# Squared queries of mixer A: turned by transposes in two parts and added up by VectorE, in place of two-column products

## What is computed

```python
q = px[..., :A_WIDTH].reshape(b, t, A_HEADS, HEAD_DIM)
q = apply_axial_rope(rms_norm(q, q_g), cos, sin)          # x tokens
...
s = jnp.einsum('bqkgd,bskd->bkgqs', qi, k_all).astype(jnp.float32) * ATTN_SCALE
p = jax.nn.softmax(s, axis=-1).astype(v_all.dtype)
o = jnp.einsum('bkgqs,bskd->bqkgd', p, v_all)
...
qc = rms_norm((hc @ w_in[:, :A_WIDTH]).reshape(b, lc, A_HEADS, HEAD_DIM), q_g)   # context tokens
```

## Time and profile before

| | |
|---|---|
| median of 3 runs | 1588.56 us (1588.26 to 1594.45) |
| profiled execution, its own time | 1596.21 us |
| its span in the trace | 1594.5 us |
| TensorE busy | 1527.1 us, 96% of the span |
| VectorE, ScalarE, GpSimd busy | 47%, 40%, 43% |
| mean granted TensorE clock | 0.98 of full speed |

### The profile page before, as it was taken

The page is one execution under the profiler, slowest core; times in us unless marked ns, Lnnn a source line. Parts: engine busy times, 40 slices in busy tenths (PEclk is TensorE's granted clock), DMA queues, the critical chain, the costliest instruction groups (busy, mean ns, idle before and its releaser), DMA issues.

```text
span 1594.5 us, 25191 instructions
## 1 busy us (share of the span) xinstructions
PE 1527.1 (96%) x10002; PEld 1231.2 (77%) x10002; DVE 743.1 (47%) x1639; ACT 636.4 (40%) x1337; POOL 686.2 (43%) x661
## 2 busy tenths in 40 slices
PE   5899999999898999999999899999999999999997
PEld 3777777677687888787877677878787877777887
DVE  4435554445534434434355464733332654455154
ACT  3335444444532533333334453434332344444331
POOL 2534444344432533433334445444353535555462
PEclk8999999999999999999999899999999999999999
DMA  9120111112023222222221222213121221111222
GB/s 396 40 80 31 50 54 54 54 58 76 1 99 114 80 73 87 106 80 80 104 83 54 106 87 80 80 53 106 54 79 54 106 106 44 64 54 54 79 86 74
DMA packets 23140, 128.21 MB, mean 80 GB/s; under 512 B 2416, under 2 KB 4592, under 8 KB 9072
## 3 DMA queue, kind: packets, MB, share of 16 engines
q1 hardware_dynamic: 22880, 126.35, 21.9%
q10 hardware_dynamic: 144, 0.26, 0.1%
HBM read 124.50 MB, written 2.10 MB: 79 GB/s over the span
## 4 chain that ended last, share of the span: by engine, by line
PE 84%; DVE 6%; POOL 3%; ACT 3%; issue 2%; DMA 1%; SPq 0%; POOLq 0%; DVEq 0%; ACTq 0%
PE PS L1525 16%; PE PS L1527 16%; PE PS L1526 15%; PE PS L1615 7%; PE PS L1605 6%; PE PS L1641 6%; PE PS L1518 3%; PE PS L1520 3%; PE PS L1519 3%; PE PS L1695 1%; PE PS L1687 1%; POOL WL L2557 1%; DMA XC<-in_xt 1%; PE PS L1538 1%; DVE AR L2354 1%
## 5 line engine op out<-in xcount | busy, mean ns | idle before, releaser
L2557 POOL TENSOR_TENSOR WL<-W,WH 128x512 fp32r<-128x512 f32 x304 | 402.2, 1337 | 322.9 <-ACT WH L1798 322.7
L1525 PE MATMUL PS<-HX,WH 128*128 128x512 f32 (+1 forms) x1008 | 411.8, 408 | 7.4 <-POOL WL L2557 3.6
L1527 PE MATMUL PS<-HX,WL 128*128 128x512 f32 (+1 forms) x1008 | 391.4, 388 | 0.0
L1526 PE MATMUL PS<-LX,WH 128*128 128x512 f32 (+1 forms) x1008 | 391.3, 388 | 0.0
L1525 PEld LDWEIGHTS PS<-HX,WH 128*128 128x128 f32 x1008 | 192.6, 191 | 54.5 <-issue 13.2
L1527 PEld LDWEIGHTS PS<-HX,WL 128*128 128x128 f32 x1008 | 192.1, 191 | 40.1
L2627 POOL TENSOR_SCALAR AR<-AR,sm 128x768 f32<-128x768 f32 (+4 forms) x160 | 112.6, 708 | 249.7 <-DVE sm L2246 248.1
L1526 PEld LDWEIGHTS PS<-LX,WH 128*128 128x128 f32 x1008 | 193.1, 192 | 34.0 <-issue 2.6
L1798 ACT CAST WH<-W 128x512 fp32r<-128x512 f32 x320 | 187.0, 619 | 41.4 <-PE PS L1520 21.0
L2227 DVE TENSOR_REDUCE sm<-PS 128x1 f32<-128x512 f32 (+4 forms) x192 | 145.0, 755 | 55.2 <-PE PS L1605 51.4
L1887 ACT ACTIVATE AR<-PS,sm 128x768 f32<-128x768 f32 (+4 forms) x160 | 114.9, 722 | 104.3 <-DVE sm L2232 86.1
(11 more groups left out here) (286 smaller groups left out, 2485.4 us busy)
## 6 DMA issues: line engine op xcount, KB each, us to landing
W<-in_wu SPq DMA_DIRECT2D x98, 1024.0 KB, 4.8
AR<-in_wu SPq DMA_DIRECT2D x8, 1024.0 KB, 11.5
AR<-in_biasb SPq DMA_DIRECT2D x32, 256.0 KB, 2.6
XX<-in_xt SPq DMA_DIRECT2D x2, 1024.0 KB, 6.2
XC<-in_xt SPq DMA_DIRECT2D x1, 1024.0 KB, 14.5
out<-XX SPq DMA_DIRECT2D x2, 512.0 KB, 3.0
out<-XX SPq DMA_DIRECT2D x4, 256.0 KB, 2.2
C<-in_cc SPq DMA_DIRECT2D x1, 770.5 KB, 8.6
```

The lines of the kernel that those rows point to most:

```text
L1525: e.matmul(o, wh, xh, start=(k == 0), stop=False)
L1526: e.matmul(o, wh, xl, start=False, stop=False)
L1527: t = e.matmul(o, wl, xh, start=False, stop=(k == 7))
L2557: e.tensor_tensor(WL[:, d, a:z], W[:, n % 2, a:z], WH[:, d, a:z].bitcast(F32), ALU.subtract).then_inc(*s_wl_pool.by(n, q))
```

## The change

The six products with two columns of ones go. In their place `qtmp` is turned tile by tile, so that tokens lie on the partitions and the 128 features of both heads along the free axis, and VectorE adds up each head's 64 squares straight from the bank. The work is in two parts, j = 0 for the four x tiles and j = 1 for the two context tiles. Each part takes a turn of the ring of its own, and its bank is freed by VectorE's adding (`s_qadd`).

In `fill_a` part 0 is named at k = 0 of the gate's x group, part 1 at k = 2, and the rotation moves from 3 to 4. In the lead-in of pair 0 both parts stand where the sums stood, and so the banks of the items behind them move on by one.

```diff
-        def query_sums(pair, pr):
-            aqps[pair, "sums"] = bank(pr.take(("aqs", pair), (s_qvar, (pair,))))
-            do("a_query_sums", pair)
+        def query_sums(pair, j, pr):
+            aqps[pair, "sums", j] = bank(pr.take(("aqs", pair, j), (s_qadd, (pair, j))))
+            do("a_query_sums", pair, j)
...
-                yield from gate_group(pair, 0, FX, {2: lambda: query_sums(pair, FC), 3: lambda: query_turn(pair, FC), 6: lambda: query_rope(pair)})
+                yield from gate_group(pair, 0, FX, {0: lambda: query_sums(pair, 0, FC), 2: lambda: query_sums(pair, 1, FC), 4: lambda: query_turn(pair, FC), 6: lambda: query_rope(pair)})
...
-        query_sums(0, vr)
+        query_sums(0, 0, vr)
+        query_sums(0, 1, vr)
...
-            def a_query_sums(pair):                    # TensorE
-                free(w, ("aqs", pair))
-                w.wait_ge(*s_qsq(pair, 1))
-                for i in range(6):
-                    t = e.matmul(aqps[pair, "sums"][:, 2 * i:2 * i + 2], qtmp[pair][:, i * 128:i * 128 + 128], c("ind"), start=True, stop=True)
-                t.then_inc(*s_qsum.by(pair))
+            def a_query_sums(pair, j):
+                free(w, ("aqs", pair, j))
+                w.wait_ge(*s_qsq(pair, j))
+                first, n = 4 * j, 4 - 2 * j
+                for i in range(n):
+                    at = 128 * (first + i)
+                    t = e.transpose(aqps[pair, "sums", j][:, 128 * i:128 * i + 128], qtmp[pair][:, at:at + 128], c("id"))
+                t.then_inc(*s_qsum.by(pair, j))
...
-            def a_query_sums(pair):                    # VectorE
-                w.wait_ge(*s_qsum(pair))
+            def a_query_sums(pair, j):
+                w.wait_ge(*s_qsum(pair, j))
                 if pair >= 2:
                     w.wait_ge(*s_exp("a", 5 * pair - 6, 1))
-                e.tensor_scalar(st[pair % 2].rearrange("p i h -> p (i h)"), aqps[pair, "sums"][:, 0:12], 1.0, 64 * EPS, ALU.mult, ALU.add).then_inc(*s_qvar.by(pair))
+                first, n = 4 * j, 4 - 2 * j
+                sums = aqps[pair, "sums", j][:, 0:128 * n].rearrange("p (i h d) -> p i h d", i=n, h=2)
+                e.tensor_reduce(st[pair % 2][:, first:first + n, :], sums, AX.X, ALU.add).then_inc(*s_qadd.by(pair, j))
+                if j:
+                    w.wait_ge(*s_qadd(pair, 1))
+                    sv = st[pair % 2].rearrange("p i h -> p (i h)")
+                    e.tensor_scalar(sv, sv, 1.0, 64 * EPS, ALU.mult, ALU.add).then_inc(*s_qvar.by(pair))
...
-            def a_query_sums(pair):                    # GpSimd
-                sv = st[pair % 2].rearrange("p i h -> p (i h)")
-                w.wait_ge(*s_qvar(pair))
-                e.tensor_tensor(sv, sv, mhalf, ALU.pow).then_inc(*s_qrs.by(pair))
+            def a_query_sums(pair, j):
+                if j:
+                    sv = st[pair % 2].rearrange("p i h -> p (i h)")
+                    w.wait_ge(*s_qvar(pair))
+                    e.tensor_tensor(sv, sv, mhalf, ALU.pow).then_inc(*s_qrs.by(pair))
```

More of the change, by code:

```diff
@@ L287, in build @@
         s_qsq, s_qraw, s_qsum, s_qvar, s_qrs = (signal("query_" + n) for n in ("squares", "raw", "sums", "var", "rs"))
+        s_qadd = signal("query_squares_added")
         s_qrot, s_qsin, s_qcos, s_qrope = (signal("query_" + n) for n in ("rotated", "sin", "cos", "roped"))
```

## The result

The changed kernel takes 1607.69 us (median of 4 runs, 1604.76 to 1607.96), beside 1590.17 us for the kernel before (4 runs, 1588.26 to 1594.45). The ratio is 1.0090 with a 95% interval of [1.0071, 1.0109], so it is slower by 14.3 us [11.3 to 17.3]; the two medians of four, taken by themselves, lie 17.5 us apart. The forecast was 1601.8 us within 1592 to 1610, and +13.2 us. Of the 5.9 us between 1601.8 and 1607.69, 2.7 to 3.0 come from the median that I added to: 14, 13 and 20 further runs of the kernel before, taken beside the experiments, have medians of 1591.23, 1591.60 and 1591.33, where the three runs at hand gave 1588.56.

A forecast was written before the change was run, and what follows sets the result against it. TensorE, 84% of the chain, was taken as the bound. Waits 9.1 + transposes ahead of the scores 2.7 - returned 0.2 + pairs 0 and 7 0.1 + clock 1.5 = +13.2 us on 1588.56: 1601.8 us, range 1592 to 1610.

The forecast's parts named there:

- The waits at bank 7: Part 0's transposes wait 1.81 us for VectorE's copy in pairs 1, 2, 3, 4 and 6: 9.1 us.
- Behind the scores: TensorE's 1.12 us less work a pair becomes a longer wait on the GpSimd and VectorE chain, bringing next to nothing.
- the term -0.2: Time returned behind the scores: 0 in pairs 1, 5, 6 and 0.2 us in pairs 2 to 4 together.
- the power is not late: Behind the scores: epsilon ready at about 180.9, before GpSimd finishes norming and starts the power at 181.27; no cost.
- VectorE's reductions: Part 0's 0.68 us falls into idle time; part 1's 0.4 us before the rotation stays inside TensorE's 1.12 us.
- Pair 7: Rotation comes behind scores 34 and their norming, while those scores start 1.5 us sooner: +0.1 us, between -0.7 and +0.9.
- Pair 0: Transposes finish sooner, but the next values wait for the bank VectorE's copy frees: 0, ends 0.7 saved and 0.3 lost.
- The clock: One fall of TensorE's clock among the five bank 7 waits: +1.5 us, with none and five falls as ends.
- The third rival: TensorE's clock falls at all five bank 7 waits, 1.5 us each: +19.2 us, 1608 us; chance 0.17.
- The saving did not arrive: Rival: no wait at bank 7 and slack in bank 5's chain, 0.68 us saved a pair, 1583 us; chance 0.06.
- The delay was not taken up: Rival: waits halved and 0.43 us returned in three pairs, +5.9 us, 1594.5 us; chance 0.17.
- The reductions did not lengthen the changed kernel: Rival: part 1 holds the power or the rotation is late, 4.9 us on top, 1606.7 us; chance 0.05.

The follow-up runs named there:

- the two last kernels: Changed kernel with part 0 in bank 6, power behind the rope, and rotation at k = 5 (1590.50 us), or rotation at k = 2 and part 1 at k = 5 (1584.99 us).
- the last kernel: Changed kernel with part 0 in bank 6, rotation at k = 2, part 1 at k = 5, power behind the rotated queries: 1584.99 us, ratio 0.9957.
- the one kernel that missed its forecast: Changed kernel with part 0 in bank 6, rotation at k = 5 instead of 4, power behind the rotated queries: 1590.50 us, ratio 1.000.

## Why the prediction was right

**The waits at bank 7** held to the tenth. Predicted was TensorE's start in pair 2 at 175.14 by the clock of before; it came at 177.53, and 2.43 us of that were there already: 175.10. It is five waits, in the five pairs named. With part 0's transposes (0.45 us) this makes 2.27 us a pair, for 1.81 + 0.45 = 2.26 predicted, and pair 5 paid its 0.45 us alone. That it is the bank is shown by the kernel with part 0 in bank 6, and that each wait costs what it lasts by the one a step later. The view of waits shows 1.62 us for each, not 1.81, because it counts from the modelled end of the product before.

**Behind the scores** the saving was lost in the chain, as said, but the term -0.2 was wrong in sign: 0.13 us a pair were added. The step that failed is "the power is not late". Epsilon was put at 0.15 us, as in the earlier trace rows, though it now reads SBUF; it took 0.67 us beside the norming and held the power back by 0.14 us. "Every tenth would count" was right: six pairs at 0.13 us, with the 0.2 us that were not returned, are 1.0 us, and 12.6 measured stands against 11.7 predicted without the clock. The waits in which it shows were sized too large: 1.6 us in pairs 1, 5 and 6 and 0.36 in 2 to 4, not 2 and 1. At the rotation TensorE lost 0.67 us by its starts, for the 0.7 predicted.

**VectorE's reductions** took 0.69 and 0.41 us (0.68 and 0.4 predicted). Doubling either left the length as it was: part 0's falls into idle time, and what TensorE waits for part 1's it would have waited for bank 5 instead. **Pair 7** gave +0.05 us for +0.1, and it is the trade that was described: 1.53 us sooner at its scores 34, and all of it lost at the next. **Pair 0** gave nothing, as taken: the values' product behind the transposes waits 0.50 us for the copy of line 2164, and from the sums to the first scores it is 17.45 us for 17.51 before.

**The clock** term, +1.5 us for one fall among the five waits, was right in size by luck. None came at the five waits. The 1.55 us of the profiled execution come from step 37, where the fall that cost nothing in the kernel before lies behind the wait and costs its full price; the prediction had no such thing. In four traces with transposes behind waits of 1.6 us (the changed kernel, the power later, either reduction twice) there is no fall in 20. With two-column products behind the same waits it was 4 in 5, in one trace. The third rival, that it falls at each of them, is out for this kernel. I had drawn on the Trainium skill, "TensorE: Matmul & The Clock Gate", Part 4 (PE-mode transpose), for it, and the traces do not bear out that use: transposes behind a wait of 1.6 us, with six more and three projection products ahead of it, did not cost the clock in these 20 places. They do not refute the rule either, since in the trace of the products one fall came behind a wait with transposes after it. What decides a fall stays open.

**The other rivals.** The saving did not arrive, since the copy ended late in all five pairs. The delay was not taken up anywhere in mixer A. The reductions did not lengthen the changed kernel.

**What stays open.** The length to step 37 leaves out what a fall of the clock costs at that step. Taken to step 38 the difference is +14.2 us for the changed kernel, +10.8 with part 0 a step later, -1.0 and -5.2 for the two last kernels, and within 0.1 us of the length for part 0 in bank 6 and for the later power in the kernel before. All of these, and +7.4 for the power later in the changed kernel, lie within the intervals of the runs, whose ratios give +14.3, +10.2, 0.0, -6.8, +7.6, -2.1 (sent again, -2.9) and +9.2. But each comes from one trace, and I did not take a second one of the kernel before. The falls of the clock behind mixer A differ from trace to trace (at 1213.4 and 1288.5 in some and not in others) without any part of the change lying there. What decides them was not tried. Nor was the last kernel's order tried with the two-column products, which would say how much of its gain the transposes bring.

## What to carry to other kernels

Work that is moved ahead in an engine's order asks for its bank ahead too: look up who frees it and when, and take the one that is free. Fewer products on the busiest engine bring nothing where a chain over slower engines is as long; shorten that chain first (here the power, which nobody needed yet), then look for the next wait (here the rotation for part 1's reduction), and the saving comes through. When a step is moved, list every queue that it passes: the one kernel that missed its forecast had a cosine behind one norming too many.

## What the runs showed of the hardware

- Behind TensorE's waits of 1.6 us followed by four transposes of 128 columns (0.66 us) the clock stayed at 2.4 GHz in 20 of 20 places in four traces. Behind the same waits followed by eight two-column passes (1.05 us) it fell to 1.2 GHz in 4 of 5 places of the one trace there is. I had feared the transposes.
- A fall of the clock cost 1.55 us or nothing at step 37, by what it covered: the output product and what follows (435.1 us, kernel after), or scores with a wait of 2 us behind them (418.0 us, kernel before).
- A VectorE instruction on 128 x 12 numbers of SBUF took 0.67 or 0.34 us beside GpSimd's norming, by when that ended, and 0.17 us where GpSimd was idle. Reading from PSUM it took 0.15 us. The reverse shows in the changed kernel with the power later, where the norming (0.91 us otherwise) took 1.27 beside VectorE's rope. Its timeline:

```profile
185.88 0.67 DVE L2209 TENSOR_TENSOR AR<-AR 128x512 f32<-128x512 f32 x1
186.06 1.27 POOL L2638 TENSOR_SCALAR AR<-AR,sm 128x768 f32<-128x768 f32 x1 [0.60 <-DVE sm L2257]
```
